# One core, a two-layer hybrid backbone with expert retrieval: the on-chip buffers laid out in another order

## The reference, cut to what matters

```
def peer(h, wq, subkeys, u_tab, v_tab):
    q = (t @ wq).reshape(-1, PEER_HEADS, 2, PEER_QDIM // 2)
    s = jnp.einsum('thpd,hpkd->thpk', q, subkeys)
    ...                                # top 16 of 128 + 128 keys for each of 8 heads
    def block(args):                   # 128 tokens at a time
        tb, ib, gb = args
        act = jax.nn.gelu(jnp.einsum('td,thkd->thk', tb, u_tab[ib]))
        return jnp.einsum('thk,thkd->td', gb * act, v_tab[ib])
```

## Time and profile before

| | us |
|---|---|
| median of 3 runs | 2312.71 |
| lowest and highest | 2308.45, 2313.47 |
| the profiled execution, its own time | 2306.4 |
| its span, first to last instruction | 2304.6 |

### The profile page before, as it was taken

How to read it: one execution, slowest core, us unless ns; L and a number is a source line. 1 busy time by engine, 2 the same in 40 slices (tenths; PEclk the granted TensorE clock), 3 DMA queues, 4 the chain that set the end, 5 groups by cost and what they waited for, 6 DMA issues and landing times.

```text
span 2304.6 us, 23920 instructions
## 1 busy us (share of the span) xinstructions
PE 2060.9 (89%) x6960; PEld 1126.1 (49%) x6960; DVE 1597.9 (69%) x3904; ACT 953.3 (41%) x2795; POOL 997.0 (43%) x868
## 2 busy tenths in 40 slices
PE   8998998999998888988999998798799978888887
PEld 7785554555564444444554554346546423333222
DVE  3865778967766668888866667855686885666654
ACT  2024444543334444444454334533554443444433
POOL 0003444344444544444445445420344545455663
PEclk9999999999999999999999999999899999999999
DMA  9979999999999999999999999986799999999997
GB/s 405 426 296 388 426 420 427 427 426 427 426 427 426 427 426 426 427 426 427 419 426 427 427 427 427 426 314 284 306 425 426 426 427 426 428 426 427 427 427 319
DMA packets 133618, 943.22 MB, mean 409 GB/s; under 512 B 14832, under 2 KB 18544, under 8 KB 19568
## 3 DMA queue, kind: packets, MB, share of 16 engines
q0 software_dynamic: 110592, 805.36, 83.2%
q1 hardware_dynamic: 22896, 136.35, 14.2%
HBM read 940.60 MB, written 1.05 MB: 409 GB/s over the span
## 4 chain that ended last, share of the span: by engine, by line
PE 38%; DMA 34%; DVE 13%; issue 6%; POOL 5%; ACT 3%; SPq 0%; POOLq 0%; DVEq 0%; ACTq 0%
DMA uv<-uv_dram,stage_idx 32%; PE psum L1016 21%; PE psum L819 9%; DVE uv L1619 5%; POOL uv L1090 5%; PE psum L801 4%; PE psum L959 1%; DVE h L1321 1%; DMA uv<-in_dram 1%; DMA uv<-ada_dram 1%; ACT diag L1264 1%; PE psum L991 1%; PE psum L734 1%; ACT small L1260 1%; DVE work L1427 1%
## 5 line engine op out<-in xcount | busy, mean ns | idle before, releaser
L1016 PE MATMUL psum<-uv,diag 128*128 128x512 f32 x3072 | 1438.7, 611 | 185.1 <-ACT diag L1264 176.7
L1090 POOL DMA_INDIRECT uv<-uv_dram,stage_idx x768 | 965.2, 1257 | 1013.3 <-PE psum L1016 773.1
L1619 DVE CUSTOM_DVE_ANT_0 uv<-uv,h 128x1024 f32<-128x1024 f32 x768 | 932.8, 1225 | 521.6 <-DMA uv<-uv_dram,stage_idx 512.2
L1016 PEld LDWEIGHTS psum<-uv,diag 128*128 128x128 f32 x3072 | 567.1, 193 | 943.8 <-issue 522.8
L1258 ACT ACTIVATE small<-small 128x1 f32<-128x1 f32 x768 | 155.1, 202 | 1016.9 <-DVE small L1619 1015.8
L1264 ACT ACTIVATE diag<-const,small 128x128 f32<-128x128 f32 x768 | 308.4, 402 | 25.1
L819 PE MATMUL psum<-hT,wring 128*128 128x256 f32 (+1 forms) x1344 | 270.9, 355 | 0.0
L819 PEld LDWEIGHTS psum<-hT,wring 128*128 128x128 f32 x1344 | 233.5, 191 | 60.8 <-issue 36.4
L1260 ACT ACTIVATE small<-small,gw 128x1 f32<-128x1 f32 x768 | 226.2, 295 | 24.9
L1076 POOL COPY stage_idx<-idx 128x8 uint32<-128x8 uint32 x96 | 31.6, 329 | 264.2 <-DVE idx L1590 263.6
L1110 ACT ACTIVATE work<-psum 128x256 f32<-128x256 f32 (+2 forms) x127 | 48.3, 383 | 130.1 <-PE psum L819 100.6
(11 more groups left out here) (220 smaller groups left out, 1276.9 us busy)
## 6 DMA issues: line engine op xcount, KB each, us to landing
uv<-ada_dram SPq DMA_DIRECT2D x27, 1024.0 KB, 19.3
wring<-wq_dram SPq DMA_DIRECT2D x26, 1024.0 KB, 11.3
wring<-in_dram SPq DMA_DIRECT2D x23, 1024.0 KB, 9.1
uv<-uv_dram,stage_idx POOLq DMA_INDIRECT x768, 21.2
uv<-in_dram SPq DMA_DIRECT2D x11, 1024.0 KB, 23.2
uv<-ada_t_dram SPq DMA_DIRECT2D x10, 1024.0 KB, 25.8
wring<-ada_dram SPq DMA_DIRECT2D x9, 1024.0 KB, 23.0
uv<-out_w_dram SPq DMA_DIRECT2D x4, 1024.0 KB, 21.0
```

Source lines behind the costliest of these rows:

```text
L1016: last = mm(acc[:, b, :], diag[:, s % DIAGS, :], uv[:, s % RING, D + 512 * b:D + 512 * (b + 1)], start=(c == 0), stop=(c == NSEL - 1))
L1090: nc.gpsimd.indirect_dma_start(out=uv[:, r, :], out_offset=None, in_=tables[stage // 2], in_offset=bass.IndirectOffsetOnAxis(ap=places[:, ...
L1619: v.tensor_tensor_reduce(out=uv[:, r, 0:D], in0=uv[:, r, 0:D], in1=h2[:, row_of[stage], t, :], scale=1.0, scalar=0.0, op0=ALU.mult, op1=AL ...
```

## The change

The diff moves lines that make buffers and changes nothing else. The ring `uv`, the weight places `wring`, the activations and the other large buffers, all of them multiples of 1,024 bytes long, come first, then `const` (8,400 bytes), and then the small ones. In the words of the change, each of the large ones begins at a multiple of 1024 bytes.

```
+        uv = sb("uv", [P, RING, 2 * D])
+        wring = sb("wring", [P, WRING, BLK_W])
+        x = sb("x", [P, 2 * TT, D])
+        h2 = sb("h2", [P, 2, TT, D])
+        hT = sb("hT", [P, KC, TOK])
+        work = sb("work", [P, 8704])
+        vx = sb("vx", [P, TT, MIX])
+        wst = sb("wst", [P, 8 * P])
+        gate_mix = sb("gate_mix", [P, D])
+        gate_peer = sb("gate_peer", [P, D])
+        keys = sb("keys", [P, 2, SUB_W])
+        diag = sb("diag", [P, DIAGS, P])
         const = sb("const", [P, W_CONST])
-        wst = sb("wst", [P, 8 * P])
         ones = sb("ones", [P, P])
-        x = sb("x", [P, 2 * TT, D])
...
-        gate_mix = sb("gate_mix", [P, D])
-        gate_peer = sb("gate_peer", [P, D])
-        wring = sb("wring", [P, WRING, BLK_W])
-        keys = sb("keys", [P, 2, SUB_W])
-        hT = sb("hT", [P, KC, TOK])
-        h2 = sb("h2", [P, 2, TT, D])
...
-        uv = sb("uv", [P, RING, 2 * D])
-        diag = sb("diag", [P, DIAGS, P])
...
-        work = sb("work", [P, 8704])
...
-        vx = sb("vx", [P, TT, MIX])
```

## The result

The changed kernel takes 2339.47 us (median of 4 runs, 2338.05 to 2341.19) against 2310.58 us for the kernel before (4 runs, 2307.8 to 2313.47): ratio 1.0125, 95% interval 1.0108 to 1.0143. That is 28.9 us slower. The forecast was 2312, within 2304 to 2320, with 0.85 on no change; it was wrong.

What follows compares the result with a forecast made beforehand. The prediction took DMA transfers as the first bound, with TensorE close behind. Its four parts summed 0 + 0 + 0 + 0 against the profiled 2306.4 us; shifted to the runs' median, the forecast was 2312 us, range 2304 to 2320.

Steps and rivals of the forecast that it cites:

- The bound: Whole kernel: DMA full in 33 of 40 slices, 1901 us, with TensorE close at 89%; transfer price acts on time first.
- The addresses: On-chip buffers: the ring moves from a multiple of 256 to 128 above one; no multiples of 1,024 arise.
- Part 1: Transfers into the ring and `wring`: price for a megabyte unchanged, 0 us, with bounds of 7.6 us more or less.
- The bound of 0.4%: Transfer price into `wring`: its share 11.6% is rounded to 0.05, 0.4% of the price, 7.6 us over 1901 us.
- The first rival: Transfers into the ring: off a multiple of 256, each packet pays for one more piece; at most +7.6 us, 2320; chance 0.06.
- the third rival: Transfers or matmuls: better alignment of the ring's neighbours or `work` and `x` makes them cheaper; -7.6 us, 2305; chance 0.06.
- The page's rule: DMA descriptors: cut at 256-byte boundaries, an off-boundary start pays for bytes before it; on the destination 1.6%, 30 us, near 2343.
- Parts 2 to 4: TensorE matmuls, VectorE's `dot`, ScalarE and GpSimd: operand addresses do not change their times; 0 us each.
- meeting operands: VectorE: large buffers agree in low address bits and `dot` goes to its present maximum; +7.5 us, 2320; chance 0.03.
- paying alignment: Transfers or matmuls become cheaper through better-aligned buffers; -7.6 us, 2305; chance 0.06.

## Why the prediction was wrong, step by step

**The bound was right.** DMA is full in 33 slices of 40, and a change of its price goes into the time nearly whole: 1.5% of 1901 us is 29 us, measured 28.9. That TensorE is close behind gave no cover against a slower transfer, and its part of the chain fell from 38% to 26%.

**The addresses were right.** That the ring leaves a multiple of 256 and that no multiple of 1,024 arises was worked out beforehand, and runs with the ring on and off the boundary confirm that this one fact decides.

**Part 1 failed.** "Offsets of 0, 192 and 208 cost the same, and 128 lies between them, so I take 0." The rows were read correctly, but neither showed the load that was coming: in the earlier trace rows 11% of the bytes went off the boundary, and in the earlier trace rows 106 of 187 packets did, close together in two microseconds, behind rows on it. The change puts every row off it, all the time. The bound of 0.4% was the rounding of a share; it bounded the price in a mixture and not that of the case that was coming. What was put at 0 measured 38.48 - 37.90 = 0.58 us for a megabyte. The kernel with the ring at 192 is the direct refutation: it costs 1.0138. The first rival had the right place and direction, but its price was capped by the same wrong bound (2320), and with 0.06 it had far too little weight. (That the ring is "three quarters of all use", in the third rival, is too low: the gathers alone are 805.36 of 943.22 MB, 85%.)

**The page's rule.** The Trainium skill, "DMA: Bandwidth & Descriptors", section "How a descriptor splits into AXI transactions", gave 2343, and the prediction set it aside for one row. The time, 2339.5, and the 256-byte boundary agree with the rule. Its arithmetic does not carry over to a destination: by it, an estimate, 64, 128 and 192 bytes would raise the price by 0.8%, 1.6% and 2.3%, and the runs show 1.5%, 1.6% and 1.5% (38.47, 38.49 and 38.46 against 37.90). That the sum came out near the measured time is thus in part luck of the offset 128. And a source off the boundary, of which it speaks, costs 0.0% here (0.9991 to 1.0010), if the tensor itself begins on a multiple of 256.

**Parts 2 to 4 held.** 379 and 592 ns for the matmuls, 1225 for `dot`, 401 for the diagonal; equal low bits of the ring and `h2` cost nothing. GpSimd's issue has a median of 1122 ns against 1094, and its part of the chain is 4% against 5%. The rivals of meeting operands and of paying alignment are out: all on 256, and all on 1,024, measure as before.

## What to carry to other kernels

Where DMA is the pace, let the buffers into which most bytes are written begin at true multiples of 256 bytes, and look at the built addresses, since what lies ahead of the first buffer shifts them all; a wider alignment brought nothing. A cost read from a few odd transfers among many ordinary ones is no bound for the case in which all are odd. Nor is a short stretch in which they are alone: here two microseconds (28 to 29.5 us) and even six (34.5 to 41 us) showed nothing, and only the five after them (41 to 46 us) the full price. Look at how long the load lasts, or make the run in which it always does. When a row and a stated rule disagree, ask whether the row shows the same load before the rule's chance is set near nothing.

## What the runs showed of the hardware that I had not expected

When all rows of 8,192 bytes are written to addresses off a multiple of 256 bytes in the on-chip memory, a megabyte costs 1.5% more (38.48 against 37.90 us of engine time), about the same at 64, 128 and 192 above one. With five of eleven rows off it the gathers cost next to nothing more (37.93), with eight 38.20. The price also depends on what went before: a stretch in which 84 of 90 packets were off the boundary was free behind rows that were on it (37.8), and the same packets at the same addresses cost 39.0 behind rows that were not. Reading from HBM at 128 bytes off costs nothing, as far as the tensor's own start is a multiple of 256. A start off a multiple of 64 adds perhaps 0.1 us for a megabyte more.
